# Attention scores of a hybrid decoder layer from high and low fp32r parts of keys and queries, in three passes, in place of fp32 products

## The chip, the cores and the metric

The kernel runs on one core of one Trainium2 chip. The metric is the device time of one execution in microseconds (us). The engines are called as the profile calls them: PE is TensorE (PEld its weight loads), DVE is VectorE, ACT is ScalarE, POOL is GpSimd and SP is SyncE. Times of single instructions come from one profiled execution.

## What is computed

One decoder layer over 16 meta tokens and 256 tokens of width 2048. A combined input projection feeds stick-breaking attention (16 heads of 64), a pooling mixer and a convolution module; their outputs are normalised, joined and projected, and a SwiGLU network follows. The change touches the scores of the attention alone, the line with `z` below.

```python
u = rmsnorm(h, pre_mix_g[i])
proj = u @ w_in[i]
q, k, v, u_pool, u_conv = jnp.split(proj, splits, axis=-1)
...
# stick_breaking_attention, with q scaled by dh ** -0.5
z = jnp.einsum('bqhd,bkhd->bhqk', q_blk, kf)
mask = (key_pos[None, :] < q_pos[:, None]) & (key_pos[None, :] >= 0)
log_not_beta = jnp.where(mask, -jax.nn.softplus(z), 0.0)
later = lax.cumsum(log_not_beta, axis=3, reverse=True) - log_not_beta
weights = jnp.where(mask, jnp.exp(jax.nn.log_sigmoid(z) + later), 0.0)
return jnp.einsum('bhqk,bkhd->bqhd', weights, vf)
...
h = h + rmsnorm(merged @ w_out[i], post_mix_g[i])
u = rmsnorm(h, pre_ffn_g[i])
ff = (jax.nn.silu(u @ w_gate[i]) * (u @ w_up[i])) @ w_down[i]
h = h + rmsnorm(ff, post_ffn_g[i])
```

## The kernel before

**Weights in chunks.** All weights stream through four slots of 128 x 1024 values. For each chunk SP loads `raw`, ACT rounds it to fp32r as `w_hi` (L561), DVE subtracts to get `w_lo` (L910, "the weight split"), and PE forms each product from three fp32r matmuls, high by high, high by low and low by high (L1377, L1379 and L1380 in the projections, L1666 to L1668 in the output projection, L1706 to L1708 in the feed-forward). ACT and DVE run a hand-written loop over chunk numbers `q`, the same on both: each turn begins with the split of chunk `q` (on DVE a piece of an earlier head pair may stand first), and then come the pieces of other work that fall due at that `q`. ACT's split of chunk `q` waits until PE has used chunk `q-4`. PE has its own order of chunks, with `side_work(q)` ahead of chunk `q`.

**The attention.** The heads come in four groups of four. A group takes 12 chunks of the projection: values, then queries, then keys. PE accumulates them in PSUM banks 2 and 3, 4, and 0 and 1. ACT copies the queries, scaled (L689, signals `q_kept`), and the keys (L694, signals `k_kept`) to SBUF as fp32. Two heads lie in the two halves of the 128 partitions. While PE goes on with the next group's projection, it does the attention of the group, two heads at a time: eight pairs in all. For one pair these steps follow each other, each some chunks after the other: `scores` on PE (L1524), the mask on DVE (L953), three ACT steps and three DVE steps for the softplus and its high and low parts (L957 to L963), the sums over later keys on PE (L1538, L1543, L1545), the log weights on DVE (L970), an exponential on ACT, and `values` on PE (L1558).

**The scores.** The 272 keys lie in three tiles of 128 (padded), and a tile is needed only for the queries behind it, so the three tiles have 256, 144 and 16 query columns. For each tile the two heads follow each other, the first with partitions 0 to 63 of keys and queries, the second with 64 to 127, into banks 5 and 6. The first block of a group stands one chunk after the group's last key chunk has been followed by one more chunk of PE work; in DVE's loop this is the turn in which it would mask the result.

**Other work near it.** DVE also computes the depthwise convolution, in single taps of 128 x 256 (L1057), up to four in each turn, until the middle of the second group. L1081 and L1086 scale and split the pooling output. POOL clears the padding of the key and value buffers (L519, L520 for the first buffer, L528, L529 for the second), and adds up squares for the norms (L524 to L535).

Of the kernel before, what the change touches and what calls it, by code (L numbers as in the profile page):

```python
# [18 lines left out]
F32 = mybir.dt.float32  # L19
F32R = mybir.dt.float32r  # L20
ALU = mybir.AluOpType
# [3 lines left out]
P = 128  # L25
# [3 lines left out]
CK = 4  # L29
# [7 lines left out]
def build_trunk(nc, x, meta, pre_mix_g, w_in, w_pool, pool_scale, w_dw, b_dw, conv_ln_g, conv_ln_b, w_pw,  # L37
                mix_out_g, w_out, post_mix_g, pre_ffn_g, w_gate, w_up, w_down, post_ffn_g, out):
    _, SEQ, D = x.shape
    META = meta.shape[0]  # L40
    TOK = META + SEQ
# [6 lines left out]
    DH = 64  # L48
# [112 lines left out]
    with ExitStack() as ctx:  # L161
# [3 lines left out]
        def place(nbytes):  # L165
            at = top[0]
            top[0] += nbytes
            return at

        def sb_at(name, shape, dt, at):  # L170
            return nc.alloc_sbuf_tensor_at(name, shape, dt, offset=at)

        CE = CK * BLK
        raw = sb_at("raw", [P, WSLOTS, CE], F32, place(4 * WSLOTS * CE))
# [20 lines left out]
        xs = sb_at("xs", [P, NQ, D], F32, a_xt)  # L195
        diag = xs[:, 0, 0:NQ * P].rearrange("p (m t) -> p m t", m=NQ)
# [7 lines left out]
        a_c = place(4 * 1152)  # L204
        cst = sb_at("cst", [P, 1152], F32, a_c)
        cst_r = sb_at("cst_r", [P, 1152], F32R, a_c)
# [29 lines left out]
        blk, c = carve(cst, c, P)  # L236
        r0, c = carve(cst, c, 3)
# [9 lines left out]
        assert c <= 1152  # L247
# [33 lines left out]
        qb[0], c = carve(arena, c, 2, SEQ)  # L281
        kb[0], c = carve(arena, c, 2, KPAD)
# [3 lines left out]
        qb[1], c = carve(arena, c, 2, SEQ)  # L286
        kb[1], c = carve(arena, c, 2, KPAD)
# [23 lines left out]
        def sem(name):  # L311
            return ctx.enter_context(nc.semaphore(name))
# [26 lines left out]
            sem("v_kept"), sem("q_kept"), sem("k_kept"), sem("vt_made"), sem("vt_kept"))  # L339
        z_made, zm_done, log_step, sp_done, sum_made, lw_done, wt_done, o_made, o_sq, o_hi, o_acc, o_lo = (  # L340
# [124 lines left out]
        def _(pool):  # L465
# [53 lines left out]
            pool.memset(kb[0][:, :, TOK:KPAD], 0.0).then_inc(pads0, 1)  # L519
# [8 lines left out]
            pool.memset(kb[1][:, :, TOK:KPAD], 0.0).then_inc(pads_ready, 1)  # L528
# [18 lines left out]
        def hi_view(ap):  # L547
            return ap.bitcast(F32)
# [358 lines left out]
        def _(dve):  # L907
# [5 lines left out]
            def split(q):  # L913
                split_lo(q, q % WSLOTS)
# [112 lines left out]

            for q in range(WSLOTS, Q_FFN):
                if q - SUMS - NEAR in PAIR_AT:
                    log_weights(PAIR_AT[q - SUMS - NEAR])  # L1030
                split(q)
                if q - NEAR in PAIR_AT:
                    masked(PAIR_AT[q - NEAR])
# [333 lines left out]
        def _(pe):  # L1367
# [144 lines left out]
            def scores(pr):  # L1512
                g, t = 2 * pr // HPG, 2 * pr % HPG // 2
                pe.wait_ge(k_kept, g + 1)
                pe.wait_ge(q_kept, g + 1)
                if g == 0:
                    pe.wait_ge(pads0, 2)
                if pr:
                    pe.wait_ge(lw_done, pr)
                pe.wait_ge(vt_kept, 2 * (g + 1))  # L1520
                for k, (at, t0) in enumerate(tiles_of):
                    for e in range(2):
                        half = slice(e * DH, e * DH + DH)
                        mm = pe.matmul(ps[:, 5 + e, at:at + TOK - t0], kb[g % 2][half, t, k * P:(k + 1) * P],  # L1524
                                       qb[g % 2][half, t, t0 - META:SEQ], start=k == 0, stop=k == 2,
                                       skip_group_check=True)
                mm.then_inc(z_made, 1)
# [36 lines left out]
            def side_work(q):  # L1564
# [31 lines left out]
                if q == PE_LNM:  # L1596
                    pe.wait_ge(tiles_added, 4)
                    pe.wait_ge(k_kept, (q - SC) // PER_G + 1)
                    column_sums(ps[:, 0, 0:SEQ], [sq4[:, 0, :]], lnm_made)
# [3 lines left out]
                if q in (PE_PW, PE_PW + 1):  # L1603
                    b = q - PE_PW
                    pe.wait_ge(ln_act, CT)
                    pe.wait_ge(k_kept, (PE_PW - SC) // PER_G + 1)
# [10 lines left out]
                if q == PE_SSA:  # L1617
                    pe.wait_ge(o_acc, DA // P)
                    pe.wait_ge(o_lo, DA // P)
                    pe.wait_ge(q_kept, GROUPS)  # L1620
                    for m in range(NQ):
                        mm = pe.matmul(ps[:, 4, m:m + 1], acc_o[:, m * P:(m + 1) * P], ones[:, 0:1], start=True, stop=True)
                    mm.then_inc(ssa_made, 1)

            for g in range(GROUPS):
                for b, outs in enumerate((wide(2), two(4), wide(0))):
# [5 lines left out]
                    if b == 1:  # L1632
                        if g:
                            pe.wait_ge(q_kept, g)
                    if b == 2:
                        pe.wait_ge(pu_kept, 1)
                        if g:
                            pe.wait_ge(k_kept, g)
# [32 lines left out]
            for g in range(OUT_G):  # L1671
                if g == 0:
                    pe.wait_ge(v_kept, GROUPS)
                if g == 1:
                    pe.wait_ge(k_kept, GROUPS)
# [165 lines left out]
```

## Time and profile before

| what | value |
|---|---|
| median of 3 runs | 1075.66 us (1075.64 to 1076.27) |
| profiled execution | 1075.67 us |
| its span, first to last instruction | 1073.7 us |
| PE busy | 1063.8 us, 99% |
| DVE busy | 891.5 us, 83% |
| ACT busy | 598.3 us, 56% |
| POOL busy | 31.5 us, 3% |
| granted TensorE clock | 0.999 |
| DMA | 208.06 MB, 194 GB/s mean |

The profile gives, for each instruction, its engine, its line and its start and end. Matmul records are pipelined: a record of PE is longer than the time until the next one starts, so the distance of two starts is what a matmul costs, and the record's own length is not. An fp32 matmul appears as two records of its shape, an fp32r matmul as one; both are written as f32. DVE's records overlap a little as well.

### The profile page before, as it was taken

The numbers are of one execution on the slowest core, as the hardware profiler recorded it, in microseconds if no ns is written. First come the engines' busy times: TensorE is split into PE (matmuls) and PEld (weight loads), VectorE is DVE, ScalarE is ACT, GpSimd is POOL, SyncE is SP. The second block draws the span as 40 slices with busy tenths as digits, with TensorE's granted clock in tenths as the row PEclk, the third lists the DMA queues.
The fourth block names the chain that finished last, engine by engine and source line by source line (L and its number), as shares of the span: only waits on it lengthen the run. The fifth ranks groups of instructions, "written<-read, shape, count | busy, mean of one in ns | idle before, by whom it ended". The sixth has DMA issues, their size and how long they took to land. (4 is left out here: it accounts for less than half of the span.)

```text
span 1073.7 us, 15358 instructions
## 1 busy us (share of the span) xinstructions
PE 1063.8 (99%) x5731; PEld 921.6 (86%) x5731; DVE 891.5 (83%) x1082; ACT 598.3 (56%) x735; POOL 31.5 (3%) x49
## 2 busy tenths in 40 slices
PE   9999999999999999999999999999999999999997
PEld 8999999999888888888888888888888888888885
DVE  6699987646646787898998998988989899988887
ACT  6554454736545565555565655655655555655553
POOL 6000001101000000000000000000000000000000
PEclk9999999999999999999999999999999999999999
DMA  8655535444386475756756656657656666566665
GB/s 271 216 176 166 172 105 162 135 143 135 112 309 214 140 266 185 225 188 193 223 174 195 216 180 212 195 181 231 189 185 222 223 200 197 189 208 214 208 200 196
DMA packets 113208, 208.06 MB, mean 194 GB/s; under 512 B 9184, under 2 KB 46496, under 8 KB 111856
## 3 DMA queue, kind: packets, MB, share of 16 engines
q1 hardware_dynamic: 111952, 201.49, 58.8%
q10 hardware_dynamic: 608, 4.20, 1.0%
q0 software_dynamic: 576, 1.40, 0.4%
q8 instruction: 46, 0.75, 0.3%
q14 instruction: 26, 0.21, 0.1%
HBM read 202.86 MB, written 4.19 MB: 193 GB/s over the span
## 5 line engine op out<-in xcount | busy, mean ns | idle before, releaser
L561 ACT ACTIVATE w_hi<-raw 128x1024 fp32r<-128x1024 f32 x321 | 337.1, 1059 | 259.0 <-PE ps L1708 153.0
L910 DVE TENSOR_TENSOR w_lo<-raw,w_hi 128x1024 fp32r<-128x1024 f32 x321 | 389.6, 1226 | 84.0 <-ACT w_hi L561 83.4
L1706 PE MATMUL ps<-w_hi,uf 128*128 128x512 f32 x524 | 205.3, 392 | 0.1
L1708 PE MATMUL ps<-w_hi,uf 128*128 128x512 f32 x524 | 204.1, 389 | 0.0
L1707 PE MATMUL ps<-w_lo,uf 128*128 128x512 f32 x524 | 203.9, 389 | 0.0
L1377 PE MATMUL ps<-u,w_hi 128*128 128x272 f32 (+1 forms) x544 | 158.8, 292 | 0.0
L1379 PE MATMUL ps<-u,w_hi 128*128 128x272 f32 (+1 forms) x544 | 155.9, 287 | 0.0
L1380 PE MATMUL ps<-u,w_lo 128*128 128x272 f32 (+1 forms) x544 | 155.7, 286 | 0.0
L841 ACT CAST t_hi<-tx 128x1024 fp32r<-128x1024 f32 x92 | 96.4, 1053 | 67.7 <-DVE tx L1202 56.4
L1708 PEld LDWEIGHTS ps<-w_hi,uf 128*128 128x128 f32 x524 | 98.4, 188 | 20.6
L1706 PEld LDWEIGHTS ps<-w_hi,uf 128*128 128x128 f32 x524 | 98.4, 188 | 20.5 <-issue 0.5
L1707 PEld LDWEIGHTS ps<-w_lo,uf 128*128 128x128 f32 x524 | 98.4, 188 | 20.0
L1213 DVE TENSOR_TENSOR t_lo<-tx,t_hi 128x1024 fp32r<-128x1024 f32 x92 | 108.2, 1218 | 0.0
L1377 PEld LDWEIGHTS ps<-u,w_hi 128*128 128x128 f32 x544 | 102.4, 188 | 0.4
L1379 PEld LDWEIGHTS ps<-u,w_hi 128*128 128x128 f32 x544 | 102.5, 188 | 0.2
L1380 PEld LDWEIGHTS ps<-u,w_lo 128*128 128x128 f32 x544 | 102.5, 188 | 0.0
L1706 PE MATMUL ps<-w_hi,ffn 128*128 128x512 f32 x256 | 99.7, 389 | 0.0
L1708 PE MATMUL ps<-w_hi,ffn 128*128 128x512 f32 x256 | 99.6, 389 | 0.0
L1707 PE MATMUL ps<-w_lo,ffn 128*128 128x512 f32 x256 | 99.6, 389 | 0.0
L1206 DVE TENSOR_TENSOR tx<-raw,tx 128x1024 f32<-128x1024 f32 x46 | 56.4, 1226 | 4.7
L1707 PEld LDWEIGHTS ps<-w_lo,ffn 128*128 128x128 f32 x256 | 48.1, 188 | 10.0
L1708 PEld LDWEIGHTS ps<-w_hi,ffn 128*128 128x128 f32 x256 | 48.1, 188 | 9.9
(277 smaller groups left out, 1473.2 us busy)
## 6 DMA issues: line engine op xcount, KB each, us to landing
raw<-in_w_gate SPq DMA_DIRECT2D x176, 256.0 KB, 3.0
raw<-in_w_up SPq DMA_DIRECT2D x176, 256.0 KB, 3.5
raw<-in_w_down SPq DMA_DIRECT2D x88, 512.0 KB, 4.2
raw<-in_w_in SPq DMA_DIRECT2D x72, 512.0 KB, 3.6
raw<-in_w_out SPq DMA_DIRECT2D x32, 512.0 KB, 4.7
arena<-in_x SPq DMA_DIRECT2D x2, 1024.0 KB, 6.2
arena<-in_x ACTq DMA_DIRECT2D x2, 1024.0 KB, 8.7
out<-h2rows SPq DMA_DIRECT2D x2, 1024.0 KB, 5.5
```

What stands on the lines that cost most here:

```text
L561: act.activation(w_hi[:, slot, :], raw[:, slot, :], ACT.Copy).then_inc(hi_done, 1)
L841: act.copy(t_hi[:, 2 * h:2 * h + 2, :], tx[:, 2 * h:2 * h + 2, :]).then_inc(t_hi_done, 1)
L910: dve.tensor_tensor(w_lo[:, slot, :], raw[:, slot, :], hi_view(w_hi[:, slot, :]), ALU.subtract).then_inc(lo_done, 1)
L1206: dve.tensor_tensor(tx[:, 2:4, :], raw[:, at[0]:at[0] + 2, 0:DCOLS], tx[:, 1:2, :].to_broadcast([P, 2, DCOLS]), ALU.add).then_inc(t_made, 1)
L1213: dve.tensor_tensor(t_lo[:, 2 * h:2 * h + 2, :], tx[:, 2 * h:2 * h + 2, :], hi_view(t_hi[:, 2 * h:2 * h + 2, :]), ALU.subtract).then_inc(t ...
L1377: pe.matmul(outs[m], w_hi[:, slot, at], x_hi, start=start and not (one_bank and m), stop=False, skip_group_check=True)
L1379: pe.matmul(outs[m], w_hi[:, slot, at], x_lo, start=False, stop=False, skip_group_check=True)
L1380: mm = pe.matmul(outs[m], w_lo[:, slot, at], x_hi, start=False, stop=last and k == len(kts) - 1, skip_group_check=True)
L1706: pe.matmul(o, a[0], b[0], start=start, stop=False)
L1707: pe.matmul(o, a[0], b[1], start=False, stop=False)
L1708: return pe.matmul(o, a[1], b[0], start=False, stop=stop)
```

## The change

The scores are no longer fp32 products. Keys and queries are kept as fp32r (their high parts, written by the same two ACT copies), and DVE makes their low parts from the PSUM result minus the high part: `qb_lo` in the turn after the last query chunk, `kb_lo` in the turn after the last key chunk, right behind the weight split of that turn. `scores` then adds three passes (high keys by high queries, high keys by low queries, low keys by high queries), each over three tiles, two heads in turns: 18 fp32r matmuls in place of 6 fp32 ones. PE waits for `q_low` and `k_low` wherever it waited for `q_kept` and `k_kept`, in front of the scores and before it overwrites the banks. The low parts lie in memory that held the scaled input rows. The padding of the fp32r buffers is made by copies of a small zero tile on POOL, four of them with one fill, in place of two fills. Constants take 896 bytes more, which moves the buffers behind them.

```diff
@@ placing
+        kb_lo = [sb_at(f"kb_lo{i}", [P, 2, KPAD], F32R, a_xt + 2 * i * D) for i in range(2)]
+        qb_lo = [sb_at(f"qb_lo{i}", [P, 2, SEQ], F32R, a_xt + 4 * D + 2 * i * D) for i in range(2)]
...
-        qb[0], c = carve(arena, c, 2, SEQ)
-        kb[0], c = carve(arena, c, 2, KPAD)
+        qb[0], _ = carve(arena_r, c, 2, SEQ)
+        kb[0], c = carve(arena_r, c + 2 * SEQ, 2, KPAD)
...
@@ POOL
             pool.wait_ge(glu_done, 2)
-            pool.memset(kb[0][:, :, TOK:KPAD], 0.0).then_inc(pads0, 1)
+            pool.memset(zeros, 0.0).then_inc(zeros_made, 1)
+            pool.wait_ge(zeros_made, 1)
+            pool.tensor_copy(kb[0][:, :, TOK:KPAD], zeros).then_inc(pads0, 1)
+            pool.wait_ge(u_lo, KT)
+            for i in range(2):
+                pool.tensor_copy(kb_lo[i][:, :, TOK:KPAD], zeros).then_inc(pads_low, 1)
             pool.memset(vb[0][:, :, TOK:KPAD], 0.0).then_inc(pads0, 1)
...
             pool.wait_ge(pn_done, PT)
-            pool.memset(kb[1][:, :, TOK:KPAD], 0.0).then_inc(pads_ready, 1)
+            pool.tensor_copy(kb[1][:, :, TOK:KPAD], zeros).then_inc(pads_ready, 1)
...
@@ DVE
+            def q_lo(g):
+                dve.wait_ge(q_kept, g + 1)
+                dve.wait_ge(u_lo, KT)
+                if g >= 2:
+                    dve.wait_ge(z_made, HPG // 2 * (g - 1))
+                dve.scalar_tensor_tensor(qb_lo[g % 2][:, :, :], ps[:, 4, :].rearrange("p (m t) -> p m t", m=2), DH ** -0.5,
+                                         hi_view(qb[g % 2]), ALU.mult, ALU.subtract).then_inc(q_low, 1)
+
+            def k_lo(g):
+                dve.wait_ge(k_kept, g + 1)
+                if g >= 2:
+                    dve.wait_ge(z_made, HPG // 2 * (g - 1))
+                dve.tensor_tensor(kb_lo[g % 2][:, :, 0:TOK], ps[:, 0:2, 0:TOK], hi_view(kb[g % 2][:, :, 0:TOK]),
+                                  ALU.subtract).then_inc(k_low, 1)
+
             for q in range(WSLOTS, Q_FFN):
                 if q - SUMS - NEAR in PAIR_AT:
                     log_weights(PAIR_AT[q - SUMS - NEAR])
                 split(q)
+                if Q_ATT <= q - 4 < Q_OUT:
+                    g, b = (q - 4 - Q_ATT) // PER_G, (q - 4 - Q_ATT) % PER_G
+                    if b == 2 * CK - 1:
+                        q_lo(g)
+                    if b == 3 * CK - 1:
+                        k_lo(g)
                 if q - NEAR in PAIR_AT:
                     masked(PAIR_AT[q - NEAR])
...
@@ PE, scores
-                pe.wait_ge(k_kept, g + 1)
-                pe.wait_ge(q_kept, g + 1)
+                pe.wait_ge(k_low, g + 1)
+                pe.wait_ge(q_low, g + 1)
                 if g == 0:
                     pe.wait_ge(pads0, 2)
+                    pe.wait_ge(pads_low, 2)
                 if pr:
                     pe.wait_ge(lw_done, pr)
                 pe.wait_ge(vt_kept, 2 * (g + 1))
-                for k, (at, t0) in enumerate(tiles_of):
-                    for e in range(2):
-                        half = slice(e * DH, e * DH + DH)
-                        mm = pe.matmul(ps[:, 5 + e, at:at + TOK - t0], kb[g % 2][half, t, k * P:(k + 1) * P],
-                                       qb[g % 2][half, t, t0 - META:SEQ], start=k == 0, stop=k == 2,
-                                       skip_group_check=True)
+                for n, (ks, qs) in enumerate(((kb, qb), (kb, qb_lo), (kb_lo, qb))):
+                    for k, (at, t0) in enumerate(tiles_of):
+                        for e in range(2):
+                            half = slice(e * DH, e * DH + DH)
+                            mm = pe.matmul(ps[:, 5 + e, at:at + TOK - t0], ks[g % 2][half, t, k * P:(k + 1) * P],
+                                           qs[g % 2][half, t, t0 - META:SEQ], start=n == 0 and k == 0,
+                                           stop=n == 2 and k == 2, skip_group_check=True)
                 mm.then_inc(z_made, 1)
...
@@ PE, before banks are used again
-                            pe.wait_ge(q_kept, g)
+                            pe.wait_ge(q_low, g)
...
-                            pe.wait_ge(k_kept, g)
+                            pe.wait_ge(k_low, g)
```

On PE, at the first block of scores (the first pair of the first group). Before, with one product of the projection ahead of it:

```order
L1380 MATMUL ps<-u,w_lo 128x272
L1524 MATMUL ps<-arena 128x256 [waits pads0,vt_kept,q_kept,k_kept]
L1524 MATMUL ps<-arena 128x256
L1524 MATMUL ps<-arena 128x144 x2
L1524 MATMUL ps<-arena 128x16 x2
```

The same place after the change; `arena_r` holds the high parts of keys and queries:

```order
L1412 MATMUL ps<-u,w_lo 128x272
L1558 MATMUL ps<-arena_r 128x256 [waits pads_low,pads0,vt_kept,q_low,k_low]
L1558 MATMUL ps<-arena_r 128x256
L1558 MATMUL ps<-arena_r 128x144 x2
L1558 MATMUL ps<-arena_r 128x16 x2
L1558 MATMUL ps<-qb_lo_66,arena_r 128x256 x2
L1558 MATMUL ps<-qb_lo_66,arena_r 128x144 x2
L1558 MATMUL ps<-qb_lo_66,arena_r 128x16 x2
L1558 MATMUL ps<-arena_r,kb_lo_64 128x256 x2
L1558 MATMUL ps<-arena_r,kb_lo_64 128x144 x2
L1558 MATMUL ps<-arena_r,kb_lo_64 128x16 x2
```

Six products have become eighteen, and the block now waits for the low parts.

On DVE, the four turns that lead to the first block. Before:

```order
L910 TENSOR_TENSOR w_lo<-raw,w_hi 128x1024 [waits hi_done]
L1057 SCALAR_TENSOR_TENSOR arena<-arena,cst 128x256 [waits tap_done] x4
L1081 SCALAR_TENSOR_TENSOR arena<-arena,cst 128x256 [waits rp_done]
...
L910 TENSOR_TENSOR w_lo<-raw,w_hi 128x1024 [waits hi_done]
L1057 SCALAR_TENSOR_TENSOR arena<-arena,cst 128x256 [waits tap_done] x4
L910 TENSOR_TENSOR w_lo<-raw,w_hi 128x1024 [waits hi_done]
L953 TENSOR_TENSOR arena<-ps,arena 128x832 [waits z_made]
```

After:

```order
L921 TENSOR_TENSOR w_lo<-raw,w_hi 128x1024 [waits hi_done]
L1044 SCALAR_TENSOR_TENSOR qb_lo_66<-ps,arena_r 128x512 [waits u_lo,q_kept]
L1089 SCALAR_TENSOR_TENSOR arena<-arena,cst 128x256 [waits tap_done] x4
L1113 SCALAR_TENSOR_TENSOR arena<-arena,cst 128x256 [waits rp_done]
...
L921 TENSOR_TENSOR w_lo<-raw,w_hi 128x1024 [waits hi_done]
L1089 SCALAR_TENSOR_TENSOR arena<-arena,cst 128x256 [waits tap_done] x4
L921 TENSOR_TENSOR w_lo<-raw,w_hi 128x1024 [waits hi_done]
L1051 TENSOR_TENSOR kb_lo_64<-ps,arena_r 128x2x272 [waits k_kept]
L964 TENSOR_TENSOR arena<-ps,arena 128x832 [waits z_made]
```

The query operation has come in behind one split, the key operation behind the split four turns later, ahead of the mask.

## Rows read from the trace of the kernel before

**Rows 1.** The profile page: busy time of the engines, and TensorE's granted clock in 40 slices
```profile
PE 1063.8 (99%) x5731; PEld 921.6 (86%) x5731; DVE 891.5 (83%) x1082; ACT 598.3 (56%) x735; POOL 31.5 (3%) x49
PEclk9999999999999999999999999999999999999999
```

**Rows 2.** Waits of PE, first of three: line, releaser: us, times, longest
```profile
PE ps L1419 <- POOL cst L469: 1.2, 1, 1.2
...
```

**Rows 3.** One line's instructions: ns min/median/max, first and last start (us), forms
```profile
L1524 PE MATMUL ps<-arena x96: 176/282/480, 130.8 to 285.6; 64*128 64x256 f32 x32, 64*128 64x144 f32 x32, 64*128 64x16 f32 x32
...
L1589 PE MATMUL ps<-arena,side x8: 377/379/381, 101.4 to 102.9; 128*128 128x256 f32 x8
```

**Rows 4.** Timeline of PE at the first block: start, us, engine, line, out<-in, count
```profile
130.77 1.07 PE L1524 MATMUL ps<-arena 64*128 64x256 f32 x12
...
131.31 0.54 PE L1524 MATMUL ps<-arena 64*128 64x144 f32 x8
...
131.78 0.39 PE L1377 MATMUL ps<-u,w_hi 128*128 128x272 f32 x1
132.01 0.29 PE L1379 MATMUL ps<-u,w_hi 128*128 128x272 f32 x1
132.13 0.29 PE L1380 MATMUL ps<-u,w_lo 128*128 128x272 f32 x1
```

**Rows 5.** Timeline of weight loads, 130.77 to 130.90
```profile
130.77 0.30 PEld L1524 LDWEIGHTS ps<-arena 64*128 64x128 f32 x4
```

**Rows 6.** Timeline of weight loads in the sums over later keys, 141.75 to 142.50
```profile
141.79 0.19 PEld L1543 LDWEIGHTS ps<-arena_r 128*128 128x128 f32 x1
...
142.46 0.19 PEld L1377 LDWEIGHTS ps<-u,w_hi 128*128 128x128 f32 x1
```

**Rows 7.** Timeline of PE, products of 256 columns
```profile
143.05 0.28 PE L1379 MATMUL ps<-u,w_hi 128*128 128x256 f32 x1
...
143.52 0.29 PE L1380 MATMUL ps<-u,w_lo 128*128 128x256 f32 x1
```

**Rows 8.** Groups of instructions on DVE: count, busy us, mean ns, idle before
```profile
L994 DVE SCALAR_TENSOR_TENSOR ysb<-ps,cst,ysb 128x512 f32<-128x512 f32 x8 | 5.7, 744 | 0.5 <-PE ps L1668 0.5
L1040 DVE TENSOR_TENSOR arena<-arena 128x544 f32<-128x544 f32 x2 | 1.5, 726 | 1.6 <-ACT arena L670 1.6
```

**Rows 9.** Timelines of DVE and of weight loads, where PE waits for a split
```profile
16.99 1.22 DVE L910 TENSOR_TENSOR w_lo<-raw,w_hi 128x1024 fp32r<-128x1024 f32 x1
...
18.27 0.19 PEld L1480 LDWEIGHTS ps<-u,w_hi 128*128 128x128 f32 x1 [0.49 <-DVE w_lo L910]
```

**Rows 10.** Timeline of DVE before the first block
```profile
117.25 1.66 DVE L1057 SCALAR_TENSOR_TENSOR arena<-arena,cst 128x256 f32<-128x256 f32 x4
...
120.41 1.21 DVE L910 TENSOR_TENSOR w_lo<-raw,w_hi 128x1024 fp32r<-128x1024 f32 x1
...
129.71 1.21 DVE L910 TENSOR_TENSOR w_lo<-raw,w_hi 128x1024 fp32r<-128x1024 f32 x1
```

**Rows 11.** Timeline of ACT: the query copy of group one, the key copy of two
```profile
115.76 0.58 ACT L689 ACTIVATE arena<-ps 128x512 f32<-128x512 f32 x1
...
172.67 0.60 ACT L694 COPY arena<-ps 128x544 f32<-128x544 f32 x1
```

**Rows 12.** Timelines of DVE and PE at the first blocks of groups two and four
```profile
172.79 1.23 DVE L910 TENSOR_TENSOR w_lo<-raw,w_hi 128x1024 fp32r<-128x1024 f32 x1 [2.23 <-ACT w_hi L561]
...
174.55 1.07 PE L1524 MATMUL ps<-arena 64*128 64x256 f32 x12
...
268.58 1.23 DVE L910 TENSOR_TENSOR w_lo<-raw,w_hi 128x1024 fp32r<-128x1024 f32 x1 [2.44 <-ACT w_hi L561]
...
270.07 1.07 PE L1524 MATMUL ps<-arena 64*128 64x256 f32 x12
```

**Rows 13.** Timelines of POOL and DVE
```profile
120.55 0.29 POOL L528 MEMSET arena<- 128x224 f32 x1 [11.28 <-DVE arena L1081]
...
167.68 1.75 DVE L910 TENSOR_TENSOR w_lo<-raw,w_hi 128x1024 fp32r<-128x1024 f32 x1
```

More of the change, by code:

```diff
@@ L173, in build_trunk @@
         CE = CK * BLK
+        CST = 1152 + 224
         raw = sb_at("raw", [P, WSLOTS, CE], F32, place(4 * WSLOTS * CE))
@@ L195, in build_trunk @@
         xs = sb_at("xs", [P, NQ, D], F32, a_xt)
+        kb_lo = [sb_at(f"kb_lo{i}", [P, 2, KPAD], F32R, a_xt + 2 * i * D) for i in range(2)]
+        qb_lo = [sb_at(f"qb_lo{i}", [P, 2, SEQ], F32R, a_xt + 4 * D + 2 * i * D) for i in range(2)]
+        assert 8 * KPAD <= 2 * D and NQ == 2
         diag = xs[:, 0, 0:NQ * P].rearrange("p (m t) -> p m t", m=NQ)
@@ L203, in build_trunk @@
         side = sb_at("side", [P, KT * SEQ], F32, a_y)
-        a_c = place(4 * 1152)
-        cst = sb_at("cst", [P, 1152], F32, a_c)
-        cst_r = sb_at("cst_r", [P, 1152], F32R, a_c)
+        a_c = place(4 * CST)
+        cst = sb_at("cst", [P, CST], F32, a_c)
+        cst_r = sb_at("cst_r", [P, CST], F32R, a_c)
         a_ff = place(4 * FT * 2 * SEQ)
@@ L236, in build_trunk @@
         blk, c = carve(cst, c, P)
+        zeros, c = carve(cst, c, 2, KPAD - TOK)
         r0, c = carve(cst, c, 3)
@@ L246, in build_trunk @@
         r2c, c = carve(cst, c, NQ)
-        assert c <= 1152
+        assert c <= CST
         V_PRE, V_MIX, V_FFN = 0, KT, 2 * KT
@@ L285, in build_trunk @@
         over = c
-        qb[1], c = carve(arena, c, 2, SEQ)
-        kb[1], c = carve(arena, c, 2, KPAD)
+        qb[1], _ = carve(arena_r, c, 2, SEQ)
+        kb[1], c = carve(arena_r, c + 2 * SEQ, 2, KPAD)
         vb[1], c = carve(arena, c, 2, KPAD)
@@ L339, in build_trunk @@
             sem("v_kept"), sem("q_kept"), sem("k_kept"), sem("vt_made"), sem("vt_kept"))
+        q_low, k_low, pads_low, zeros_made = sem("q_low"), sem("k_low"), sem("pads_low"), sem("zeros_made")
         z_made, zm_done, log_step, sp_done, sum_made, lw_done, wt_done, o_made, o_sq, o_hi, o_acc, o_lo = (
@@ L1597, in side_work @@
                     pe.wait_ge(tiles_added, 4)
-                    pe.wait_ge(k_kept, (q - SC) // PER_G + 1)
+                    pe.wait_ge(k_low, (q - SC) // PER_G + 1)
                     column_sums(ps[:, 0, 0:SEQ], [sq4[:, 0, :]], lnm_made)
@@ L1605, in side_work @@
                     pe.wait_ge(ln_act, CT)
-                    pe.wait_ge(k_kept, (PE_PW - SC) // PER_G + 1)
+                    pe.wait_ge(k_low, (PE_PW - SC) // PER_G + 1)
                     for m in range(2):
@@ L1619, in side_work @@
                     pe.wait_ge(o_lo, DA // P)
-                    pe.wait_ge(q_kept, GROUPS)
+                    pe.wait_ge(q_low, GROUPS)
                     for m in range(NQ):
@@ L1674, in _ @@
                 if g == 1:
-                    pe.wait_ge(k_kept, GROUPS)
+                    pe.wait_ge(k_low, GROUPS)
                 for s in range(OC if g < OUT_G - 1 else 0):
```

## The prediction

> **What bounds the kernel now.** I read the header of the profile page first. PE is busy for 1063.8 of 1073.7 us, at a granted clock of nine tenths or more in all forty slices [rows 1]. The list of waits agrees: PE waits three times in the whole run, 1.2 us at the most, all before its first projection chunks are through, and never in the attention stage [rows 2]. So every microsecond of PE work that is added is a microsecond of time, and so is every wait that reaches PE. Work on the other engines is free until PE waits for it. The profiled execution took 1075.67 us (its span and 2.0 us around it), the median of the runs is 1075.66, so a change of the span can be added to either.
>
> Then I looked at one block of scores, at what stands between its first weight load and the next product's, and third at what VectorE does just before the first block of each group of heads, since the change puts two new operations there.
>
> **Part 1, the products.** There are eight blocks, one for each pair of heads. A block has 6 fp32 products now, which the trace shows as 12 records, and 18 fp32r products after the change [rows 3]. The block at 130.77 lasts until the next product begins at 131.78: 1.00 us when read to the nanosecond of the start and end times, 1.01 by the rounded rows [rows 4].
>
> Where does the 1.00 go? An fp32 product of 256 columns over the full array is two records, and 8 such records start from 101.4 to 102.9, 1.5/7 = 0.214 us apart: 0.213 us of streaming each, two cycles a column at 2.4 GHz [rows 3]. In the scores block four such records, two heads by two passes, fit in the 0.54 us from 130.77 to 131.31, which is one exposed weight load of 0.107 us and two times 0.216 [rows 4]. So the two heads, which lie in different halves of the array's rows, run side by side. Their weights do too: four loads of 186 ns lie within 0.30 us, so the second pair starts 0.11 us after the first and the heads of a pair together [rows 5]. The block is then: first load 0.107; streams 2 x 0.213 and 2 x 0.120 = 0.667; the load for the second 16-column pass, which its 7 to 13 ns of streaming can't hide, 0.107; and about 0.115 before the next product's load may start. That makes 1.00.
>
 A step of 256 columns takes 0.118 us (four steps from 143.05 to 143.52) [rows 7]. Nine steps: load 0.107, then 3 x 0.118 + 5 x 0.111 = 0.91 to the last step's start, then 0.115: 1.13 us. Against 1.00 that is **+0.13 us a block, +1.0 us for eight**. Three passes at a quarter of fp32's cycles save no time here: the streams shrink from 0.69 to 0.52 us, but the tiles are too short to cover nine loads. Bounds: loads 0.107 apart as in rows 5 give +0.09 a block (+0.7); steps of 0.125, what a 272-column product takes at 132.01, give +0.22 (+1.8).
>
> **Part 2, the waits.** PE may now start a group's first block only after VectorE has made the low parts of keys and queries (q_low, k_low), where it waited for ScalarE's copies. VectorE's low part of the keys stands behind the weight split of the same turn; each costs a PE wait if it ends after the time at which PE comes. The key operation (128x544, PSUM and SBUF to SBUF) is of the size of the 726 ns gating product, the query operation (128x512) of the 744 ns one that also reads PSUM [rows 8]; back to back an operation starts 0.08 us before its forerunner's record ends, so the query one adds 0.66 in a full queue. From VectorE's end to PE's load takes 0.05 us: the split begun at 16.99 for 1.22 ends at 18.21, the load begins at 18.27 [rows 9].
>
> *First group.* VectorE is full from 117.25 to 130.92: eleven groups of its timeline, of which the first, one between and the last stand, each beginning where the last one ends less the overlap [rows 10]. ScalarE's query copy ends at 116.34 and is in time for a query operation at 117.25, and nothing between absorbs it [rows 11]. So the split that ended at 130.92 ends 0.66 later, at 131.58; the key operation starts at 131.50 and ends at 132.23; PE starts at 132.28 instead of 130.77: **+1.51 us**. What is queued behind the key operation on VectorE is the masking of the same block, which waits for PE anyway, so the chain moves with PE. Two operations cost more than one here, since the first is 4 turns away and still counts whole.
>
> *Second and third group.* VectorE was idle before the last split, so the query operation falls into idle time. The split runs 172.79 to 174.02, the key operation 173.94 to 174.67 (ScalarE's key copy is ready at 173.27), PE starts at 174.72 instead of 174.55: **+0.17** each; the third repeats the second's spacing [rows 11, 12]. *Fourth group.* Split 268.58 to 269.81, key operation to 270.46, PE at 270.51 instead of 270.07: **+0.44** [rows 12]. The four later blocks use parts that are long made. Waits: 1.51 + 0.17 + 0.17 + 0.44 = **+2.3 us**. Bounds: both operations at 0.65 and no wake-up time 1.9; and above, 0.1 more in each group and 0.5 once for GpSimd.
>
> **Part 3, what costs nothing.** ScalarE's copies are the same, rounded on the way out. GpSimd's clearing becomes one fill and three copies of 224 elements, one of the copies where a fill stands at 120.55. GpSimd's work may slow VectorE: a 1.22 us split took 1.75 at 167.68, where GpSimd was adding [rows 13]. A copy in the full stretch could thus add up to 0.5 to the first wait; I take nothing, since beside the fill at 120.55 the split took its 1.21 [rows 10]. Waits that guard banks (q_low, k_low for the next group) come eight or more chunks after the operation. The depthwise taps of the second group end 0.7 us later; no wait of PE hangs on them now [rows 2].
>
> **Sum.** 1.0 + 2.3 = +3.3 us, 1075.7 + 3.3 = **1079.0 us**, 0.3% slower; bounds of this case 0.7 + 1.9 = 2.6 and 1.8 + 3.2 = 5.0, so 1078.3 to 1080.7. A measurement of this kernel can tell about 0.2% (2.2 us) from no change.
>
> **Rivals.** *Weights load fast (ends at no change).* If fp32r weights of a 64-row tile loaded at least as fast as the columns stream, the steps would be 0.118, 0.072 and 0.02 us (streams plus the 0.011 that a 256-column product has over its own), the block 0.107 + 0.61 + 0.115 = 0.83, and eight blocks would give back 8 x 0.17 = 1.4 against 2.3 of waits: 1076.6, within 0.2%. The point from which it decides: a load under about 0.07 us. Against it: the loads 0.111 us apart in rows 6 are of fp32r data, though of 128 rows. Chance 0.10. The Trainium skill, page "TensorE: Matmul & The Clock Gate", section "Weight-path perf modes — Fast Weight Load (FWL) and DoubleRow", says that the fast load is on for 128 weight columns when the type is not FP32; were fp32r such a type, this rival would hold, but by rows 6 it is not.
>
> *The heads don't overlap in fp32r.* At one column a cycle two heads write PSUM at twice the rate that the fp32 block shows. If they went one after another, a block would have 18 loads 0.111 apart: 0.107 + 17 x 0.112 + 0.115 = 2.13, +1.13 a block, +9.0 for eight, with the waits +11.3: 1087.0. Rows 4 and 5 show overlap of streams and of loads, but in fp32 alone. Chance 0.12. The same page of the Trainium skill (section "Measured speedup vs the span model") gives tiles in different rows as concurrent with a few ns between, which speaks for the overlap.
>
> *VectorE's delay spreads.* GpSimd's copy slows the full stretch and further weight splits come late: 0.5 to 2.5 more, 1079.5 to 1081.5. For it: rows 13; against it: no PE wait on a split is in the attention stage now [rows 2]. Chance 0.06.
>
> **How the numbers follow.** Main case 0.72, at 1079.0. Left out of the range are the serial heads and little more: from 1076.6 (fast loads) to 1081.5. Slower by over 0.2% (above 1077.8): main case, serial heads and spread delay, less a little of the main case for a wait that comes out shorter: 0.82. Within 0.2%: 0.15. Faster by over 0.2% would need fast loads and no waits at all: 0.03.
>
> **What would show it.** In the profile after: a PE wait of some 1.5 us before the scores in the first group, for VectorE's key operation, and of 0.2 to 0.5 in the three others; 144 records of the scores in place of 96; the block 1.13 us from its first load to the next product's, with loads 0.11 apart in pairs. A block of 0.8 shows fast loads, one of 2.1 shows heads in series. A first wait under 1 us would mean that I read VectorE's queue wrongly.

## The result, and the profile after

| what | before | after |
|---|---|---|
| median (range, runs) | 1075.69 us (1075.64 to 1076.51, 6) | 1086.60 us (1085.88 to 1087.45, 6) |
| ratio | | 1.010, 95% interval 1.0089 to 1.0110 |
| profiled execution, its span | 1075.67 us, 1073.7 us | 1087.45 us, 1085.7 us |

The changed kernel is slower by 10.9 us, 1.0%. The prediction was 1079.0 us with a range up to 1081.5: the sign was right, the size was not, and the time lies outside the range. The header of the page after, beside [rows 1]:

```profile
PE 1073.2 (99%) x5779; PEld 925.0 (85%) x5779; DVE 897.1 (83%) x1090; ACT 599.0 (55%) x735; POOL 34.2 (3%) x52
PEclk9999999999999999999999999999999999999998
```

PE is busy 9.4 us longer, though the scores have only 48 records more. PE's waits, beside [rows 2]:

```profile
PE ps L1558 <- DVE kb_lo L1051: 1.8, 2, 1.5
PE ps L1451 <- POOL cst L475: 1.2, 1, 1.2
```

The one new wait is 1.5 us in the first group, as forecast, and 0.3 in the fourth; this view counts idle time alone, and leaves out the 0.1 us of it in the second and in the third group. By the starts of the products before the blocks, against the kernel before, the four waits cost 1.53, 0.16, 0.16 and 0.38 us. The first block on PE's timeline, beside [rows 4] (start, duration, engine, line, operation, count, and the idle time before it with its releaser):

```profile
130.54 0.29 PE L1412 MATMUL ps<-u,w_lo 128*128 128x272 f32 x1
132.29 0.51 PE L1558 MATMUL ps<-arena_r 64*128 64x256 f32 x6 [1.46 <-DVE kb_lo L1051]
132.65 0.48 PE L1558 MATMUL ps<-qb_lo,arena_r 64*128 64x256 f32 x6
132.99 0.49 PE L1558 MATMUL ps<-arena_r,kb_lo 64*128 64x256 f32 x6
133.41 0.39 PE L1409 MATMUL ps<-u,w_hi 128*128 128x272 f32 x1
...
134.28 0.43 PE L1409 MATMUL ps<-u,w_hi 128*128 128x272 f32 x1
134.50 0.43 PE L1411 MATMUL ps<-u,w_hi 128*128 128x272 f32 x1
```

The block starts at 132.29 and the next product at 133.41: 1.12 us. Then comes something that the prediction does not have. From 134.28 the same projection products start 0.22 us apart, where they were 0.12 to 0.13 apart before the wait. The windows of the same kernel (stretch, length, busy time and count of PE, PEld, DVE, ACT and POOL, then the granted clock, the DMA share and GB/s):

```profile
130.00:134.00 4.00, 2.54 (x29) 2.30 (x28) 2.71 (x5) 0.00 (x0) 0.00 (x0) 1.00 0.67 192
134.20:137.60 3.40, 3.40 (x17) 3.40 (x17) 0.97 (x3) 2.96 (x4) 0.00 (x0) 0.50 0.17 61
137.60:140.00 2.40, 2.40 (x21) 2.40 (x20) 2.33 (x3) 1.75 (x2) 0.00 (x0) 0.99 0.00 0
```

The granted clock is 0.50 for 3.4 us, the 1.2 GHz level. Before it fell, PE had stood idle for 1.5 us and had then been busy for 1.9 us, with one block and six products.

The rest is far from the scores. I laid the starts of the same PE instructions in the two traces side by side. At the end of the attention, near 286 us, the kernel after is 5.0 us late. That is 1.5 of waiting and 1.5 of clock at the first block, 0.7 in the waits of the other groups, 0.9 in the longer blocks, and 0.4 early in the output projection. The output projection adds some 1.5 (6.5 us late at 363). Over the feed-forward's gate and up products, from there to 830 us, the lateness stands still. Over the down projection it grows steadily again, to 11.6 at the last product, and 12.0 at the end of the span: between VectorE's last instruction and the end lie 3.75 us, before 3.40. These 0.35 us are in every kernel made from the changed one and in none made from the kernel before; what they are stays open. The costliest groups, with shapes kept apart (count, busy us, mean ns of one), first of the kernel before:

```profile
L1706 PE MATMUL ps<-w_hi,uf 128*128 128x512 f32 x524 | 205.3, 392 | 0.1
...
L1706 PE MATMUL ps<-w_hi,ffn 128*128 128x512 f32 x256 | 99.7, 389 | 0.0
```

and of the kernel after:

```profile
L1740 PE MATMUL ps<-w_hi,uf 128*128 128x512 f32 x524 | 205.3, 392 | 0.0
...
L1740 PE MATMUL ps<-w_hi,ffn 128*128 128x512 f32 x256 | 101.1, 395 | 0.0
...
L1700 PE MATMUL ps<-w_hi,ffn 128*128 128x512 f32 x128 | 51.2, 400 | 0.0
```

The products that take `uf` are what they were. Those that take `ffn` have records 6 ns longer. The starts tell what that costs, here the first and the last of eleven steps in the kernel after:

```profile
949.76 0.40 PE L1740 MATMUL ps<-w_hi,ffn 128*128 128x512 f32 x1
...
952.32 0.39 PE L1742 MATMUL ps<-w_hi,ffn 128*128 128x512 f32 x1
```

and in the kernel before:

```profile
949.72 0.39 PE L1706 MATMUL ps<-w_hi,ffn 128*128 128x512 f32 x1
...
952.22 0.39 PE L1708 MATMUL ps<-w_hi,ffn 128*128 128x512 f32 x1
```

By these rows the steps are 0.2327 us against 0.2273. Read to the nanosecond over the whole trace, most are 0.232 against 0.227, 5.5 ns more on average. There are 1152 such products and 96 of the same kind with `t_hi` and `t_lo`; 1248 x 5.5 ns is 6.9 us. Nothing in the diff touches them, except that the constants grew by 896 bytes and `ffn` lies behind them. In these products `ffn` gives the 128 columns that stay in the array, and the weight slots give the 512 columns that stream.

### The profile page after: what moved, and what is told of

It reads as the page before. It is cut to its first block and busy times, and to the rows that moved or that the text cites. A ratio compares the mean times of both kernels' runs of the same rounds, so it can differ in the third digit from the quotient of the medians.

```text
span 1085.7 us, 15472 instructions
## 1 busy us (share of the span) xinstructions
PE 1073.2 (99%) x5779; PEld 925.0 (85%) x5779; DVE 897.1 (83%) x1090; ACT 599.0 (55%) x735; POOL 34.2 (3%) x52
## 5 line engine op out<-in xcount | busy, mean ns | idle before, releaser
L1740 PE MATMUL ps<-w_hi,ffn 128*128 128x512 f32 x256 | 101.1, 395 | 0.0
L1742 PE MATMUL ps<-w_hi,ffn 128*128 128x512 f32 x256 | 101.0, 395 | 0.0
L1740 PEld LDWEIGHTS ps<-w_hi,ffn 128*128 128x128 f32 x256 | 48.2, 188 | 11.2
L1742 PEld LDWEIGHTS ps<-w_hi,ffn 128*128 128x128 f32 x256 | 48.3, 189 | 11.2
```

The lines of the kernel that those rows point to most:

```text
L1740: pe.matmul(o, a[0], b[0], start=start, stop=False)
L1742: return pe.matmul(o, a[1], b[0], start=False, stop=stop)
```

## Experiments

The theory after this reading: about 3.3 us are the products and waits of the forecast, 7 us are the place of `ffn`, and 1.5 us the clock. The rivals: the `ffn` products are slower for what the new scores leave behind (other PSUM use, other timing of DMAs), or for `ffn`'s own address; and the 1.5 us wait costs only itself.

**The place alone, and the change without it.** `s896` is the kernel before with `ffn` moved as the change moves it; `s1024` and `s128` move it by 1024 and 128 bytes; `a1024` is the kernel after with `ffn` moved by 1024 bytes in all.

```diff
-        a_c = place(4 * 1152)
+        a_c = place(4 * 1152 + 896)
```

```diff
-        a_c = place(4 * CST)
+        a_c = place(4 * CST + 128)
```

> The kernel before, with nothing changed but 896 bytes left empty between the constants and the ffn buffer, so that ffn and all behind it lie where they lie after the change. Theory (placement): the 6.5 us that PE loses after the scores, in products that take ffn as the stationary operand (their records 395 ns instead of 389), come from where ffn lies: 1075.7 + 6.5 = 1082.2 us, the output projection and the down projection slower, all else alike. Rival (load): those steps are slower because of what else the change does to PE or its clock; then this kernel takes 1075.7.

> The kernel before with 1024 bytes left empty at the same place. Placement, if what counts is the address within 512 or 1024 bytes: 1075.7 as before, ffn products at 389 ns. If any move of ffn costs: 1082 as with 896. Load: 1075.7.

> The changed kernel with 128 more bytes left empty, so that ffn moves by 1024 bytes in all instead of 896. Placement: the 6.5 us go, 1086.6 - 6.5 = 1080.1 us, which leaves 0.9 for the products, 2.2 for the waits and about 1.5 for PE's clock at half level after the long wait. Load: 1086.6 as before.

> The kernel before with 128 bytes left empty. A period of 512 bytes with one bad residue (that of 896, which is 384): ffn at another residue, so 1075.7. If only the old place was good: up to 1082. Load: 1075.7.

| kernel | median us | ratio to before (1076.04), 95% |
|---|---|---|
| s896 | 1083.36 | 1.0070 (1.0053 to 1.0086) |
| s1024 | 1075.86 | 1.0000 (0.9990 to 1.0010) |
| s128 | 1082.65 | 1.0062 (1.0042 to 1.0083) |
| a1024 | 1079.39 | 1.0035 (1.0020 to 1.0049) |

One changed number in the kernel before costs 7.3 us, and its trace has the same long records, here of `s896`:

```profile
L1706 PE MATMUL ps<-w_hi,uf 128*128 128x512 f32 x524 | 205.3, 392 | 0.0
...
L1706 PE MATMUL ps<-w_hi,ffn 128*128 128x512 f32 x256 | 101.0, 395 | 0.0
```

So the scores have no part in it. A move by 1024 bytes costs nothing, a move by 128 costs 6.6: distance is not what counts. The expectation for `s128` had one bad remainder in mind, that of 896 bytes, and 1075.7 us; it was wrong. With the place mended the change costs 3.35 us, 1079.39 us, where the sum of the forecast was 3.3 and 1079.0.

The 1.5 us wait is still there in `a1024`, and this time no fall of the clock follows in the profiled execution:

```profile
132.46 0.51 PE L1558 MATMUL ps<-arena_r 64*128 64x256 f32 x6 [1.47 <-DVE kb_lo L1051]
...
134.31 0.29 PE L1412 MATMUL ps<-u,w_lo 128*128 128x272 f32 x1
134.44 0.29 PE L1409 MATMUL ps<-u,w_hi 128*128 128x272 f32 x1
```

**Own address or relation to the streamed operand.** Before, the weight slots and `ffn` had the same remainder when their places are divided by 512, since every buffer between them is a multiple of 512 bytes long. `all128` moves every buffer by 128, so the relation stays; `mix` moves the slots by 128 and `ffn` by 512, so `ffn`'s own remainder by 512 stays and the relation does not. `s64` moves `ffn` by 64 alone.

```diff
+        place(128)
         raw = sb_at("raw", [P, WSLOTS, CE], F32, place(4 * WSLOTS * CE))
...
-        a_c = place(4 * 1152)
+        a_c = place(4 * 1152 + 384)
```

(`all128` has the first part alone, `mix` both; `s64` is `s896` with 64.)

> The kernel before with 128 bytes left empty ahead of all buffers: weights, inputs, constants and ffn all move by 128, and lie to each other as they did. Theory relative (products are slow when the stationary operand in ffn and the moving operand in the weight buffers lie at different residues of 512 bytes): 1075.9, ffn products at 389 ns. Theory absolute (ffn itself must lie at residue 128, as it does before and with 1024): 1082.7 as with ffn alone moved by 128, and the products from the input buffer may get slower too.

> The kernel before with 128 bytes left empty ahead of all buffers and 384 more ahead of ffn: the weight buffers and the inputs move by 128, ffn by 512. Relative: ffn now lies at another residue than the weights, so its products take 395 ns, those from the input buffer 389, about 1082.7. Absolute: ffn is at its old residue of 512, so its products take 389; if the input buffer counts in the same way, its products go to 395.

> The kernel before with 64 bytes left empty ahead of ffn. Relative placement with a tolerance of one 64-byte step: 1075.9 us, ffn products at 389 ns. Without any tolerance: 1082.7 as with 128.

Measured: `all128` 1075.99 us, ratio 1.0001 (0.9991 to 1.0011); `mix` 1082.80, 1.0065 (1.0045 to 1.0086); `s64` 1084.16, 1.0079 (1.0058 to 1.0099). The groups of `all128`, of `mix`, and of `s64`:

```profile
L1707 PE MATMUL ps<-w_hi,ffn 128*128 128x512 f32 x256 | 99.7, 389 | 0.0
```

```profile
L1707 PE MATMUL ps<-w_hi,uf 128*128 128x512 f32 x524 | 205.2, 392 | 0.0
...
L1707 PE MATMUL ps<-w_hi,ffn 128*128 128x512 f32 x256 | 101.0, 395 | 0.0
```

```profile
L1706 PE MATMUL ps<-w_hi,ffn 128*128 128x512 f32 x256 | 101.3, 396 | 0.0
```

The relation decides: differences of 0 and 1024 bytes (remainder 0 by 512) are fast; 64, 128, 384 and 896 (remainder 384) are slow. The last three cost nearly the same, 7.0 us of span each in the traces. The move by 64 costs more, 8.3 us by the medians: its `ffn` steps are 6.3 ns longer instead of 5.4. Of differences under 512 bytes only these three (64, 128, 384) were tried.

**Is it `ffn`, or any operand that stays?** `in128` moves, in the kernel before, the buffer that holds `u`, `uf` and the row sums `sums_u` by 128 bytes, and all behind it by 512, so that `ffn`, the row sums `sums_f` and the `t` buffers keep their relation to the weights.

```diff
+        place(128)
         a_in = place(4 * KT * 2 * TOK)
...
+        place(384)
         a_xt = place(4 * KT * SEQ)
```

> The kernel before with the input buffer (u and uf, and the sums in it) moved by 128 bytes, all behind it by 512, so that ffn and the t buffers keep their residue of 512 against the weight buffers. Theory (any stationary operand that lies otherwise than the moving one is slow): the products of uf with the weights in the feed-forward go from 389 to 395 ns, 524 x 3 of them, 8 us or so more, 1083.5 us; products of ffn stay at 389. Rival (only ffn's place matters, for what it holds or who writes it): 1075.9 us.

Measured: 1088.23 us, 1.0117 (1.0096 to 1.0137). Of `in128`:

```profile
L1708 PE MATMUL ps<-w_hi,uf 128*128 128x512 f32 x524 | 207.9, 397 | 0.1
...
L1708 PE MATMUL ps<-w_hi,ffn 128*128 128x512 f32 x256 | 99.7, 389 | 0.0
...
L1708 PE MATMUL ps<-t_hi,sums_f 128*128 128x512 f32 x90 | 35.3, 392 | 0.0
```

Now the products of `uf` with the weights are the long ones and those of `ffn` with the weights are not: it does not depend on which buffer gives the stationary side. The size missed. The cost is 12.4 us where the expectation had about 8. Laid beside the trace of the kernel before, the 1572 `uf` products with the weights lose 8.5 us, and the 198 others whose stationary side moved (`uf` with `t`, and `sums_u`) lose 1.5. Products of `sums_f` and `ffn` whose relation is kept lose another 1.3 us, in the first twelve places behind a misplaced one; 0.2 are lost by the last product before a misplaced one, 0.5 in the first 17 us of the run, and 0.2 in the projections.

That last 0.2 bounds the rule. In the projections the weights are the stationary side and `u` streams. Their relation was broken too, and the records are as before, first the kernel before, then `in128`:

```profile
L1377 PE MATMUL ps<-u,w_hi 128*128 128x272 f32 x416 | 121.8, 293 | 0.0
```

```profile
L1379 PE MATMUL ps<-u,w_hi 128*128 128x272 f32 x416 | 121.9, 293 | 0.0
```

Their steps grew by 0.1 ns on average, so these runs show the loss in products of 512 columns only. Whether the columns or the direction makes the difference was not tried.

**Waits apart from products.** Both from `a1024`. `waits` keeps the low parts and the waits but forms the scores by fp32 products; `products` keeps the 18 fp32r products, all from the high parts, and drops the low parts and their waits.

```diff
-                for n, (ks, qs) in enumerate(((kb, qb), (kb, qb_lo), (kb_lo, qb))):
-                    for k, (at, t0) in enumerate(tiles_of):
...
+                for k, (at, t0) in enumerate(tiles_of):
...
+                        mm = pe.matmul(ps[:, 5 + e, at:at + TOK - t0], kb[g % 2][half, t, k * P:(k + 1) * P].bitcast(F32),
```

```diff
-                pe.wait_ge(k_low, g + 1)
-                pe.wait_ge(q_low, g + 1)
+                pe.wait_ge(k_kept, g + 1)
+                pe.wait_ge(q_kept, g + 1)
...
-                for n, (ks, qs) in enumerate(((kb, qb), (kb, qb_lo), (kb_lo, qb))):
+                for n, (ks, qs) in enumerate(((kb, qb), (kb, qb), (kb, qb))):
```

> The changed kernel with ffn moved by 1024 bytes, and scores from one pass of fp32 products over the rounded keys and queries; the low parts are made and waited for but not used, so the result leaves them out. It shows the waits alone. Theory: PE waits 1.5, 0.17, 0.17 and 0.4 us before the first blocks of the groups, blocks at 1.00 us: 1076.0 + 2.2 = 1078.3, and up to 1.5 more in executions in which PE's clock falls after the long wait. Rival (the 3.35 us of the aligned kernel are mostly in the products): 1076.5 or less.

> The changed kernel with ffn moved by 1024 bytes, without the low parts: all three passes take the high parts, and PE waits for the copies as it did before. The result leaves out the low parts and counts the high product three times. It shows the 18 products alone. Theory: 8 x 0.12 = 0.9 us, 1076.9 us; no waits of PE before the scores. Rival (the waits are nothing, the products all): 1079.4. If the heads ran one after another it would be 1085.

Measured against 1075.78 us: `waits` 1078.32, +2.5 (1.0024, 1.0014 to 1.0033); `products` 1077.11, +1.3 (1.0010, 1.0001 to 1.0020). By the trace 0.86 of it is PE's lateness, from the eight blocks, and 0.35 the time at the end of the span told of above. The two add up to 3.8 where `a1024` has 3.35, within their intervals. Without those 0.35 the halves are 2.2 and 1.0, where the forecast said 2.3 and 1.0.

**Can the wait be avoided?** `fixed`, from `a1024`, puts the key's low part ahead of the weight split and takes convolution taps out of VectorE's full turns.

```diff
+        if 36 <= q <= 38:
+            many = 2
...
+                if in_att and b == 3 * CK - 1:
+                    k_lo(g)
                 split(q)
...
-                    if b == 3 * CK - 1:
-                        k_lo(g)
```

> The changed kernel with ffn moved by 1024 bytes, the low part of the keys made ahead of the weight split of its turn instead of behind it, and two depthwise taps fewer in each of the three turns before the first block (they are made later). Theory: no wait of PE is left, the 18 products remain: 1075.8 + 0.9 = 1076.7 us, within 0.2% of the kernel before. Rival (VectorE's queue is late for another reason): a wait of 0.5 us or more stays before the first block, 1077.3 or more.

Measured: 1076.95 us, +1.05 (1.0012, 1.0002 to 1.0022). VectorE, then PE, of `fixed`:

```profile
128.69 0.72 DVE L1053 TENSOR_TENSOR kb_lo<-ps,arena_r 128x544 fp32r<-128x544 f32 x1 [1.40 <-ACT arena_r L707]
129.34 1.21 DVE L923 TENSOR_TENSOR w_lo<-raw,w_hi 128x1024 fp32r<-128x1024 f32 x1
```

```profile
129.73 0.29 PE L1414 MATMUL ps<-u,w_lo 128*128 128x272 f32 x1
129.95 0.51 PE L1560 MATMUL ps<-arena_r 64*128 64x256 f32 x6
```

The low part is ready at 129.41, before PE comes, and the wait is gone, as are those of the other three groups. In those the order alone did it. In the first group two things changed at once, and they were not tried apart; by an estimate from [rows 4], [rows 8], [rows 9] and [rows 10] the order alone would have left some 0.4 us there (the key operation from 129.71 + 0.66 for 0.73 us, and 0.05 to PE, which comes at 130.77). What is left is the price of the products and the 0.35 us at the end. This is the best form of the change that I found, and it is not faster than the kernel before.

**What a wait does to the clock.** `longwait`, from `a1024`, makes the first low part four times, so that PE waits longer. `longwarm` fills that wait with 16 fp32 products of the constants into a bank that the scores then overwrite.

```diff
+                if g == 0:
+                    for i in range(3):
+                        dve.tensor_tensor(kb_lo[0][:, :, 0:TOK], ps[:, 0:2, 0:TOK], hi_view(kb[0][:, :, 0:TOK]),
+                                          ALU.subtract).then_inc(k_again, 1)
+                        dve.wait_ge(k_again, i + 1)
```

```diff
+                if pr == 0:
+                    pe.wait_ge(vt_kept, 2)
+                    for _ in range(16):
+                        pe.matmul(ps[:, 5, 0:P], ones, ones, start=True, stop=True)
```

> The changed kernel with ffn moved by 1024 bytes, in which VectorE makes the low part of the first group's keys four times in a row, so PE waits some 2.2 us longer there. Theory (a long idle time of PE makes its clock fall to 1.2 GHz, and whether it does depends on its length and place): the clock falls in all or most executions, and the products after it start 0.227 us apart instead of 0.125 for some 3.4 us: 1079.4 + 2.2 + 1.5 = 1083.1 us. Rival (the fall in the profile of the changed kernel had another cause): 1081.6 us, full clock.

> The kernel of the long wait, in which PE does 16 fp32 products of 128 columns on constants (some 3.5 us) in front of that wait, so that it waits the same time but idles little. Theory (idle time makes the clock fall): full clock in every execution, the products after the block 0.125 us apart, 1082.94 - 1.5 = 1081.4 us. Rival (the fall comes with the late scores or with what VectorE does): 1082.9 us as without them.

Measured: `longwait` 1082.94 us (+7.0, 1.0072, 1.0055 to 1.0089), `longwarm` 1081.97 (+6.2, 1.0057, 1.0040 to 1.0074). Of `longwait`, PE's timeline and a window:

```profile
134.60 0.51 PE L1564 MATMUL ps<-arena_r 64*128 64x256 f32 x6 [3.75 <-DVE kb_lo L1057]
...
136.52 0.43 PE L1417 MATMUL ps<-u,w_hi 128*128 128x272 f32 x1
136.75 0.43 PE L1418 MATMUL ps<-u,w_lo 128*128 128x272 f32 x1
```

```profile
136.00:139.40 3.40, 3.40 (x21) 3.38 (x20) 1.42 (x2) 2.04 (x3) 0.00 (x0) 0.62 0.00 0
```

and of `longwarm`:

```profile
131.75 3.74 PE L1555 MATMUL ps<-cst 128*128 128x128 f32 x32
135.68 0.51 PE L1568 MATMUL ps<-arena_r 64*128 64x256 f32 x6 [0.20 <-DVE kb_lo L1057]
...
137.03 0.29 PE L1417 MATMUL ps<-u,w_hi 128*128 128x272 f32 x1
137.16 0.29 PE L1418 MATMUL ps<-u,w_lo 128*128 128x272 f32 x1
```

```profile
136.00:140.00 4.00, 4.00 (x43) 3.98 (x40) 1.42 (x2) 1.96 (x3) 0.00 (x0) 1.00 0.00 1
```

After 3.75 us of idling the products start 0.23 apart for a while; after the filled wait they start 0.13 apart, at full clock. The block of `longwarm` begins 1.08 us later, because that execution was already 1.07 late after its first 17 us, ahead of the edit, and still its span is 0.5 us shorter (1080.7 against 1081.2): the fall costs 1.5 to 1.6 us. The median of `longwarm` is 1.0 us below that of `longwait`, where 1.5 was expected, and the two intervals overlap, so the size rests on the traces. `longwait` is 3.7 us slower than `a1024`, of which the longer wait is 2.3 and the rest, 1.4, is the clock.

Whether the 1.5 us wait of the kernel after brings a fall differs between executions: it is in the profiled one (1087.45 us), and in neither `a1024` nor `waits` when they were profiled. The six executions of the kernel after fit that, a weak sign since the kernel before has mean clocks of 0.997 to 0.999 too: two at a mean clock of 0.996 took 1087.45 and 1087.43, the others at 0.997 to 0.999 took 1085.88 to 1086.66. What tips it is open.

**Is the block bound by its loads?** `narrow`, in the kernel before, gives the third key tile 32 weight columns in place of 128 (16 hold keys; the other key columns of that tile are left out of the scores).

```diff
-                        mm = pe.matmul(ps[:, 5 + e, at:at + TOK - t0], kb[g % 2][half, t, k * P:(k + 1) * P],
+                        n = P if k < 2 else 32
+                        mm = pe.matmul(ps[0:n, 5 + e, at:at + TOK - t0], kb[g % 2][half, t, k * P:k * P + n],
```

> The kernel before, with the third key tile of the scores (16 real keys) taken with 32 weight columns instead of 128, fp32 as before. Theory (what a small tile costs is its weight load, which goes with the columns): the last load shrinks from 0.107 to 0.03 us, a block from 1.00 to 0.92, eight blocks 0.6 us: 1075.2 us. Rival (a load costs the same for any number of columns, or the change of the column group costs more): 1075.8 or more.

Measured: 1076.20 us, 1.0004 (0.9994 to 1.0013). A miss: nothing was gained, and the trace has the block longer, not shorter.

```profile
130.77 1.11 PE L1525 MATMUL ps<-arena 64*128 64x256 f32 x12
131.82 0.39 PE L1377 MATMUL ps<-u,w_hi 128*128 128x272 f32 x1
```

```profile
131.65 0.14 PEld L1525 LDWEIGHTS ps<-arena 64*32 64x32 f32 x4
131.81 0.19 PEld L1377 LDWEIGHTS ps<-u,w_hi 128*128 128x128 f32 x1
```

The block lasts 1.05 us instead of 1.00. The narrow loads are short, as expected: read to the nanosecond, the two steps start 0.028 us apart, where loads of 128 columns are 0.11 apart. But the first of them begins only at 131.65, about 0.1 after the streams of the tile before it end, where a load of the same width as the one before runs beside those streams. So the 0.1 us stands where the tile's shape changes, and the second narrow load, of the same shape as the first, does not have it. The same 0.1 us stands at both edges of every block [rows 4], where full-array and 64-row tiles meet.

## Why the prediction was right and wrong

**Products: right.** Forecast 1.13 us a block and 0.13 more than before; measured 1.12 and 0.115 to 0.12, 0.9 us over eight. All 144 records are there, 48 of each pass. PEld of the kernel after shows why:

```profile
132.51 0.19 PEld L1558 LDWEIGHTS ps<-arena_r 64*128 64x128 f32 x2
132.62 0.19 PEld L1558 LDWEIGHTS ps<-qb_lo,arena_r 64*128 64x128 f32 x2
```

Two loads, one for each head, lie within one record's length, and the next two follow 0.11 us later. A quarter of the cycles for a column saved nothing, because nine loads set the time, as forecast.

**Waits: right.** The first block began at 132.29, forecast 132.28. The four waits came to 1.53, 0.16, 0.16 and 0.38 us, forecast 1.51, 0.17, 0.17 and 0.44. `waits` and `products` measured the two terms apart, and `a1024` their sum: 1079.39 against 1079.0, +3.35 against +3.3. That the sums agree to 0.1 us is partly luck, as 0.35 us of the measured one is at the end of the span, where the forecast had nothing. Two slips in the working changed nothing: the lower bound of a block, with nine loads 0.107 apart, comes to 1.08 us, +0.08 and not +0.09, and GpSimd makes four copies, not three.

**The three rivals: all false.** The serial heads would have given 1087.0 us, nearly what was measured, and that is chance. That rival's own mark was a block of 2.1 us, and the block is 1.12 with its loads in pairs. The fast loads needed a block of 0.8; the loads of fp32r in 64-row tiles are 0.11 us apart, as slow as those of 128 rows in [rows 6]. The Trainium skill, page "TensorE: Matmul & The Clock Gate", section "Weight-path perf modes — Fast Weight Load (FWL) and DoubleRow", turns the fast load on for 128 weight columns of a type other than FP32; for fp32r this trace shows no such load. VectorE's delay did not spread: no further PE wait on a weight split appeared in the attention.

**The step that failed: "what costs nothing".** The description of the change said that the constants take 896 bytes more, which moves the buffers behind them. The part that lists the free things does not even name it, so it went in at zero, with no bound. It costs 7.3 us by `s896`, two thirds of the loss. No row of the kernel before shows it, since in its products of 512 columns the weights and `ffn` or `uf` have the good relation; but a moved buffer was an edit like any other, and its bound should have been looked for and the range kept open above. The range's upper end came from VectorE alone.

**A second, smaller term was missing.** The 1.5 us wait was priced at 1.5 us. It can also cost what the clock does afterwards, about 1.5 us more, in some executions. The profiled one is such a case; it lies 0.85 us above the median.

## What to carry to other kernels

When a buffer moves, compare the mean duration of the matmuls that read it before and after, even in stages that the change doesn't touch: here the distance of the stationary operand from the streamed one, its remainder by 512 bytes, was worth more than the change itself, and 128 bytes of padding bring it back. For matmuls with few columns count the weight loads and the changes of tile shape, not the streamed columns. Put a small operation that PE waits for ahead of the filler on its engine: this took the wait away in three groups, and in the first together with fewer taps.

## What the runs showed of the hardware

- An fp32r product of 128 x 512 starts 0.227 us after the one before when the places of its stationary and its streamed operand in SBUF have the same remainder by 512 bytes, and 0.232 to 0.233 us after it when they don't (0, 1024 and all buffers by 128: fast; 64, 128, 384 and 896: slow). In products of 256 and 272 columns, whose weights are the stationary side, a difference of 128 bytes cost nothing that shows (0.1 to 0.2 ns a step, `in128`).
- The relation is shown; why it matters is not. The traces say a little: in `s128`, `s896` and `mix` the last well-placed product before the `ffn` ones already takes 6 ns more (0.232 to 0.233 us, means of 17), as if the load of the next stationary columns met the stream of this product. But the last `ffn` product before a well-placed one is as slow as the others (0.234), while in `s64` the product before is not slow (0.226), and in `s64` and `in128` products are slower for some places behind a misplaced one. So one such load alone does not explain it.
- Two heads in different halves of the rows load and stream side by side in fp32r as in fp32: the two loads of a pair start 3 to 4 ns apart in the kernel after.
- After 1.5 us of idling the granted clock fell to 0.50, the 1.2 GHz level, for 3.4 us in one profiled execution and stayed at 1.00 in two others. After 3.75 us it fell in the profiled one, and with the same gap filled by products it stayed.
- A load of 32 weight columns takes 0.028 us, the distance of two such loads in `narrow`, but a load for a tile of another shape than the last started only about 0.1 us after the streams had ended.
